# A gate product with its tiles out of step: tile 0 ends one unit sooner, and the next row is turned amid the last unit

## The chip, the cores and the metric

The kernel runs on one core of one Trainium2 chip. Time is device time in microseconds, the median of the runs. Everything is float32; each product is made of three passes over split operands (below).

## The reference

Two stacked blocks over 256 tokens of width 1024. Block 1 has two layers. Each ends in a gated embedding, and what it gives is normed again at once by the next layer (or, after the second layer, by block 2's first feed-forward):

```python
x = x + rms_norm(ff, norm_ffn_post[i])
e = (p[i] @ w_ple_proj[i]) * jax.nn.sigmoid(x @ w_ple_gate[i])
x = x + rms_norm(e, norm_ple[i])
# next layer
h = rms_norm(x, norm_mix_pre[i + 1])
z = h @ w_in[i + 1]
```

The product `x @ w_ple_gate` is "the gate product" here, the step from one layer to the next "the seam". There are two seams.

## The kernel before

**Tiles and units.** The 256 tokens are two tiles of 128 rows, t = 0 and 1 ("rows" below are such tiles). Weights come in units of 128 x 2048 float32 (1 MB) through three slots of `raw`. ScalarE rounds a unit to its high part `whi` (`split` in ScalarE's program, L1482 and L1486), VectorE subtracts to get the low part `wlo` (`split` in VectorE's program, L2013; halves of a unit through L2019). A product is rows_high x weights_high (L660, L650), rows_high x weights_low (L629) and rows_low x weights_high (L638). TensorE's instruction for a unit and a tile is `unit_product`; for a wide unit it is 12 matmuls, four in each pass. Usually the order of the passes is high, low weights, low rows. If `rows_first` names the unit, the low rows come ahead of the low weights.

**The gate product** is `wide_job(U_PGATE, 4, ...)`: four units, each used by both tiles. The order written (t, unit) is (0,0) (0,1) (1,0) (1,1) (0,2) (0,3) (1,2) (1,3). Counted over the layer these units are 68 to 71; 72, 73, 74 and 75 are the first four units of what follows. A slot comes free for ScalarE when the last tile has used the unit three before; SyncE issues the load of a unit when the low part of the unit two before it is made.

**From gate to next row.** For each tile: sigmoid on ScalarE (`gate_e`, L1809), product with the embedding on VectorE (`embed`, L2484), then beside each other a square sum on ScalarE (`square_e`, L1519) and a product with the row of gains of the next norm on VectorE (`embed_rows`, L2489). Of tile 1 the last quarter of that product is made by GpSimd (L2893). GpSimd makes the inverse root from the sum (L2775 addition, L2776 power). VectorE combines all to the next normed row in `ht` (`next_row`, L2499). TensorE transposes it (`turn`, L698, eight transposes for a tile), ScalarE copies out the high part (L1494), VectorE the low part (L2019).

**Order around the seam.** Every engine's order is written out by hand. After the gate product TensorE does three filler transposes (`stay_warm`, L705), the turn of tile 0 of the next row, and six more fillers. Then it begins the next layer's first product. The turn of tile 1 lies inside that product: in the first layer's successor at the second unit, in the middle of its low-weight pass, after five and a half passes; in block 2's first product, whose second unit keeps the usual order of passes, after four and a half. Behind this turn TensorE waits for the whole of unit 73's low part. Its first half has a flag of its own (`seam_lo`).

VectorE's order: splits of units 70, 71 and 72 with small work between; `embed(0)`, `embed_rows(0)`, `next_row(12, 0)`; first half of 73; `embed(1)`, `embed_rows(1)`; low part of tile 0's next row; `next_row(13, 1)`; second half of 73; the residual of tile 0 (`add_embedded`); low part of tile 1's next row; half of 74; residual of tile 1; half of 74; 75.

Of the kernel before, what the change touches and what calls it, by code (L numbers as in the profile page):

```python
# [21 lines left out]
P = 128  # L22
S = 256
T = S // P
D = 1024
# [26 lines left out]
SLOTS = 3  # L52
UW = 2048
# [10 lines left out]
ACT = mybir.ActivationFunctionType  # L64
# [56 lines left out]
START_POS = START_COL + DT  # L121
START_FREQ = START_POS + T
START_WORDS = START_FREQ + ROPE // 2
WARM_SHORT, WARM_LONG, WARM_START = 6, 3, 10
AHEAD_ONE, AHEAD_TWO = 6, 3


# [133 lines left out]
def two_blocks(nc, A, out):  # L261
    ctx = ExitStack()
    with ctx:
# [12 lines left out]
        xs = sb("xs", [P, T, D])  # L276
# [107 lines left out]
        def sem(name):  # L384
            if name not in sems:
                sems[name] = ctx.enter_context(nc.semaphore(name))
            return sems[name]
# [22 lines left out]
        def u_view(buf, u, kts, cols):  # L410

            return buf[:, u % SLOTS, 0:kts * cols].rearrange("p (k n) -> p k n", k=kts)
# [184 lines left out]
        def _(pe):  # L597
            w = Place()

            def free_before(cls, k):  # L600

                _, name, n = w.read(cls, k - 2)
                pe.wait_ge(sem(name), w.at(name, n))
# [70 lines left out]
            def unit_product(u, t, kt, parts, start, stop, ready=None, by_halves=False):  # L674


                ready = ready or AT_ONCE
                if t == 0:
                    if by_halves:
                        pe.wait_ge(sem("first_hi"), w.at("first_hi", u + 1))  # L680
                    elif ready.seam:
                        unit_hi_there(u)
                    else:
                        unit_there(u)
                ready.before(t, kt)
                return product(parts, start, stop,
                               weights_lo=(lambda: low_weights_there(u, ready)) if t == 0 and ready.seam else None,
                               amid=lambda i: ready.amid(t, kt + i), rows_lo=lambda: ready.rest(t, kt), rows_first=kt in ready.rows_first and t == 0,
                               half=(lambda: unit_hi_there(u)) if t == 0 and by_halves else None,
                               by_turns=w.layer == 0 and t == 0 and by_halves)  # L690
# [16 lines left out]
            def rows(k, name, n, src=None, ahead=AHEAD_TWO, first_turned=False, rows_first=(), in_parts=None,  # L707
                     part_there=None, second_turned=False):

                src = ht if src is None else src
                turned = [first_turned, second_turned]

                def turn_half(g):
                    turned[0] = True
                    turn(k + g, lambda j: src[:, 0, (4 * g + j) * P:(4 * g + j + 1) * P], 4)

                def turn_tile(t):
                    if not turned[t]:  # L720
                        turned[t] = True
                        pe.wait_ge(sem(name), w.at(name, n + t + 1))
                        for g in range(2):
                            turn(k + 2 * t + g, lambda j: src[:, t, (4 * g + j) * P:(4 * g + j + 1) * P], 4)

                def before(t, kt):
                    if kt == 0:
                        turn_tile(t)
                    if kt % 4 == 0:
                        turn_hi_there(k + 2 * t + kt // 4)  # L730

                def amid(t, kt):
                    if kt == ahead:
                        turn_tile(1)
                        if in_parts is not None and t == 0:
                            unit_there(in_parts)

                def rest(t, kt):
                    if kt % 4 == 0:
                        was_read("turn", k + 2 * t + kt // 4)  # L740
                turn_tile.half = turn_half
                return Ready(before, amid, rest, True, rows_first, in_parts, part_there), turn_tile

            def wide_job(u, units, hf, hi, lo, ready=None, late=None):

                for j0 in range(0, units, 2):
                    for t in range(T):
                        for j in range(j0, min(j0 + 2, units)):  # L750
                            if j == 0:
                                free_before("half", hf + t)
                            if late and (j, t) == (units - 1, T - 1):
                                late()
                            vh, vl = u_view(whi, u + j, 2, D), u_view(wlo, u + j, 2, D)
                            outs = [ps[:, 4 + 2 * t + n, :] for n in range(2)]
                            last = unit_product(u + j, t, 2 * j,
                                                [(outs, hi[:, 2 * j + k, t * P:(t + 1) * P], lo[:, 2 * j + k, t * P:(t + 1) * P],
                                                  [vh[:, k, n * 512:(n + 1) * 512] for n in range(2)],
                                                  [vl[:, k, n * 512:(n + 1) * 512] for n in range(2)]) for k in range(2)],  # L760
                                                j == 0, j == units - 1, ready)

                            if j == units - 1:
                                last.then_inc(sem("half_done"), 1)
                            elif t == T - 1:
                                last.then_inc(sem("used"), 1)

            def ffn(u, gu, tn, hf, ready, between=None, by_columns=False):
                def gate_up(u, gu, ready=None):
# [259 lines left out]
            def layer1():  # L1029
# [206 lines left out]
                                   True, True, amid=(lambda i: turn_first(0) if i == 1 else None) if t == 0 else None)  # L1236
                    last.then_inc(sem("half_done"), 1)
                was_read("half", HF_PROJ)
                ready_embed, turn_embed = rows(TN_PLE, "x_ready", 2, xs)
                ffn(U_FFN, 0, TN_HID, HF_DOWN, ready, lambda: turn_embed(0))  # L1240
                wide_job(U_PGATE, 4, HF_PG, act_hi, act_lo, ready_embed)
                stay_warm(WARM_LONG)
                rows(len(TURN1) + TN_MIX, "h_ready", PER_LAYER["h_ready"])[1](0)
                stay_warm(WARM_SHORT)

            for n, s in enumerate(counted[0::2]):
                pe.sem_inc(s, BASE)
# [213 lines left out]
        def _(act):  # L1461
# [165 lines left out]
            def layer1():  # L1627
# [174 lines left out]
                square_half(11, HF_DOWN + 1, fold[:, 1:2])  # L1802
                split(1)
                turned_rows_hi(TN_PLE, (1,))
                split(2)

                def gate_e(t):
                    half_there(HF_PG + t)
# [7 lines left out]
                gate_e(0)  # L1816
                square_e(12, 0)
                split(1)
                gate_e(1)
                turned_rows_hi(len(TURN1) + TN_MIX, (0,))  # L1820
                square_e(13, 1)
                split(1)
                turned_rows_hi(len(TURN1) + TN_MIX, (1,))
# [170 lines left out]
        def _(dve):  # L1994
# [232 lines left out]
            def layer1():  # L2227
# [284 lines left out]
                nc.vector.tensor_tensor(row_next[:, :], gains[:, 0, :], gains[:, 1, :], ALU.mult)\  # L2512
                    .then_inc(sem("v_link"), 1)
                links[0] += 1
                split(1)
                embed(0)
                dve.wait_ge(sem("v_link"), w.at("v_link", links[0]))
                embed_rows(0)
                next_row(12, 0)
                u = done[0]  # L2520
                assert u == UNITS1 + 1
                dve.wait_ge(sem("hi"), w.at("hi", u + 1))
                kept = [(slice(None), u % SLOTS, slice(c * UW // 2, (c + 1) * UW // 2)) for c in range(2)]
                rest(wlo[kept[0]], raw[kept[0]], whi[kept[0]]).then_inc(sem("seam_lo"), 1)
                embed(1)
                embed_rows(1, 3 * D // 4)
                turned_rows_lo(len(TURN1) + TN_MIX, 0)
                next_row(13, 1)
                rest(wlo[kept[1]], raw[kept[1]], whi[kept[1]]).then_inc(sem("lo"), 1)
                done[0] += 1  # L2530
# [562 lines left out]
```

## Time and profile before

| | |
|---|---|
| median of 3 runs | 1860.77 us (1860.44 to 1861.28) |
| profiled execution | 1860.99 us |
| its span, first to last instruction | 1859.2 us |
| granted TensorE clock, mean | 0.999 |
| TensorE, VectorE, ScalarE, GpSimd busy | 99%, 65%, 53%, 9% |

The profile is of one execution. Its lines give start, length and engine; PE is TensorE's matmuls, PEld its weight loads, DVE VectorE, ACT ScalarE, POOL GpSimd, SP SyncE. Times in brackets are idle time in front of an instruction and who ended it. A gap between weight loads tells when TensorE could go on better than the matmuls' modelled ends do.

### The profile page before, as it was taken

To read this page: it belongs to the slowest core of one execution; us is meant where nothing else is said; L and a number is where in the kernel's file an instruction comes from. 1 tells how busy PE (TensorE), PEld (TensorE's weight loads), DVE (VectorE), ACT (ScalarE), POOL (GpSimd) and SP (SyncE) were. 2 spreads that over 40 slices of the span, in tenths; PEclk is the share of its full clock that TensorE was granted. 3 is DMA by queue.
4 is the path that set the end of the run, shared out by engine and by line. 5 is a ranking of instruction groups with operands and counts; after the bars stand their busy time and mean duration, and the time that the engine had idled before them with its cause. 6 is when DMAs were issued, how large, how long until landed. Compare 5 with 4: busy or idle time off the path is not lost.

```text
span 1859.2 us, 26803 instructions
## 1 busy us (share of the span) xinstructions
PE 1847.4 (99%) x9608; PEld 1544.2 (83%) x9608; DVE 1209.4 (65%) x1493; ACT 991.3 (53%) x1299; POOL 161.7 (9%) x260
## 2 busy tenths in 40 slices
PE   9999999999999999999999999999999999999998
PEld 7878888888877888888888887788888888778887
DVE  7875665668876666667755646666666556576555
ACT  6774454456675454445544556644454444575443
POOL 8100010002210010000100021000020000100000
PEclk9999999999999999999999999999999999999999
DMA  7345566554435465555556454465565555535553
GB/s 260 111 155 189 179 204 203 194 181 156 155 121 187 170 215 201 179 185 192 189 201 203 165 196 149 154 203 184 181 200 183 182 199 192 182 114 171 184 188 113
DMA packets 204724, 333.18 MB, mean 179 GB/s; under 512 B 10976, under 2 KB 149856, under 8 KB 204640
## 3 DMA queue, kind: packets, MB, share of 16 engines
q1 hardware_dynamic: 201376, 320.82, 51.5%
q0 software_dynamic: 3120, 11.02, 1.8%
q8 instruction: 48, 0.79, 0.2%
q14 instruction: 36, 0.29, 0.0%
q10 hardware_dynamic: 144, 0.26, 0.0%
HBM read 331.01 MB, written 1.05 MB: 179 GB/s over the span
## 4 chain that ended last, share of the span: by engine, by line
PE 96%; DVE 1%; DMA 1%; issue 1%; ACT 0%; POOL 0%; SPq 0%; POOLq 0%; DVEq 0%; ACTq 0%
PE ps L819 21%; PE ps L660 19%; PE ps L638 19%; PE ps L629 19%; PE ps L837 11%; PE ps L698 3%; PE ps L930 2%; PE ps L942 2%; PE ps L958 2%; DMA raw<-w_in_dram 1%; DVE eb L2484 0%; POOL stat L2776 0%; DVE wlo L2019 0%; PE ps L795 0%; ACT prob L1519 0%
## 5 line engine op out<-in xcount | busy, mean ns | idle before, releaser
L2013 DVE TENSOR_TENSOR wlo<-raw,whi 128x2048 fp32r<-128x2048 f32 (+1 forms) x294 | 664.4, 2260 | 180.4 <-ACT whi L1486 176.6
L1486 ACT ACTIVATE whi<-raw 128x2048 fp32r<-128x2048 f32 (+3 forms) x306 | 569.7, 1862 | 136.2 <-PE ps L638 133.2
L819 PE MATMUL ps<-act,whi 128*128 128x512 f32 x1728 | 403.6, 390 | 0.0
L819 PEld LDWEIGHTS ps<-act,whi 128*128 128x128 f32 x1728 | 323.5, 188 | 66.5
L1549 ACT ACTIVATE hid<-ps 128x512 f32<-128x512 f32 x54 | 32.2, 597 | 396.1 <-PE ps L837 396.1
L2085 DVE TENSOR_TENSOR hid<-ps,hid 128x512 f32<-128x512 f32 x54 | 37.4, 692 | 314.1 <-ACT hid L1549 314.1
L837 PEld LDWEIGHTS ps<-act,wlo 128*128 128x128 f32 x1728 | 214.5, 192 | 4.2
L837 PE MATMUL ps<-act,wlo 128*128 128x256 f32 x1728 | 215.8, 283 | 0.0
L629 PE MATMUL ps<-wlo,act 128*128 128x512 f32 (+2 forms) x768 | 207.6, 385 | 0.8 <-DVE wlo L2013 0.7
L660 PE MATMUL ps<-whi,act 128*128 128x512 f32 (+2 forms) x760 | 201.9, 386 | 0.2
L638 PE MATMUL ps<-whi,act 128*128 128x512 f32 (+2 forms) x760 | 198.7, 381 | 0.6 <-DVE act L2019 0.6
L638 PEld LDWEIGHTS ps<-whi,act 128*128 128x128 f32 x760 | 140.1, 188 | 28.9 <-DVE act L2019 1.4
L629 PEld LDWEIGHTS ps<-wlo,act 128*128 128x128 f32 x768 | 139.7, 188 | 29.1 <-DVE wlo L2013 1.4
L660 PEld LDWEIGHTS ps<-whi,act 128*128 128x128 f32 x760 | 138.4, 188 | 27.6 <-issue 0.8
L2775 POOL TENSOR_TENSOR stat<-stat,eps 128x1 f32<-128x1 f32 x43 | 23.3, 542 | 1438.1 <-ACT prob L1519 1437.9
L660 PE MATMUL ps<-whi,hid_hi 128*128 128x512 f32 x496 | 134.5, 393 | 0.0
L629 PE MATMUL ps<-wlo,hid_hi 128*128 128x512 f32 x496 | 133.4, 390 | 0.0
L638 PE MATMUL ps<-whi,hid_lo 128*128 128x512 f32 x496 | 132.7, 389 | 0.0
L629 PEld LDWEIGHTS ps<-wlo,hid_hi 128*128 128x128 f32 x496 | 93.0, 188 | 19.9
L638 PEld LDWEIGHTS ps<-whi,hid_lo 128*128 128x128 f32 x496 | 93.1, 188 | 19.4
L660 PEld LDWEIGHTS ps<-whi,hid_hi 128*128 128x128 f32 x496 | 89.2, 189 | 15.3
L1541 ACT ACTIVATE hid_hi<-hid 128x512 fp32r<-128x512 f32 x54 | 34.2, 632 | 70.5 <-PE ps L638 70.5
(267 smaller groups left out, 1958.7 us busy)
## 6 DMA issues: line engine op xcount, KB each, us to landing
raw<-ffn_w_gate_dram SPq DMA_DIRECT2D x88, 512.0 KB, 3.7
raw<-ffn_w_up_dram SPq DMA_DIRECT2D x88, 512.0 KB, 4.7
raw<-ffn_w_down_dram SPq DMA_DIRECT2D x88, 512.0 KB, 4.3
raw<-w_in_dram SPq DMA_DIRECT2D x62, 512.0 KB, 4.5
raw<-w_ffn_gate_dram SPq DMA_DIRECT2D x44, 512.0 KB, 3.7
raw<-w_ffn_up_dram SPq DMA_DIRECT2D x44, 512.0 KB, 4.7
raw<-w_ffn_down_dram SPq DMA_DIRECT2D x44, 512.0 KB, 4.4
raw<-a_w_qkv_dram SPq DMA_DIRECT2D x24, 512.0 KB, 4.3
```

What stands on the lines that cost most here:

```text
L629: last = nc.tensor.matmul(o, hi, a, start=False, stop=last_pass and stop and i == len(parts) - 1)
L638: last = nc.tensor.matmul(o, lo, a, start=False, stop=last_pass and stop and i == len(parts) - 1)
L660: nc.tensor.matmul(o, hi, a, start=start and i == 0, stop=False)
L698: last = nc.tensor.transpose(bank[0:rows, j * P:(j + 1) * P], src(j), ident[:, :])
L819: nc.tensor.matmul(ps[:, 2 * g + j, :], vh[:, k, g, j * P:(j + 1) * P], both[:, 4 * half + k, :, :], start=half == 0 and k == 0, stop=False)
L837: last = nc.tensor.matmul(ps[:, 2 * g + j, 0:S], vl[:, k, g, j * P:(j + 1) * P], act_hi[:, 4 * half + k, :], start=False, stop=half == 1 a ...
L930: return nc.tensor.matmul(ps[:, sc % 2, t * S:t * S + cols], q[t], k[:, 0:cols], start=True, stop=True)
L942: last = nc.tensor.transpose(ps[:, bank, kt * S + t * P:kt * S + (t + 1) * P], prob[:, sc % PROBS, t, kt * P:(kt + 1) * P], ident[:, :])
L958: return nc.tensor.matmul(o, v[:, kt], probT[:, sc % 2, kt, c0:S], start=kt == 0, stop=kt == T - 1)
L1486: nc.scalar.activation(whi[:, u % SLOTS, half:words], raw[:, u % SLOTS, half:words], ACT.Copy)\
L2013: nc.vector.tensor_tensor(wlo[:, u % SLOTS, 0:words], raw[:, u % SLOTS, 0:words], whi[:, u % SLOTS, 0:words].bitcast(F32), ALU.subtract)\
L2085: nc.vector.tensor_tensor(dst[:, :, :], ps[:, 2 * g:2 * g + 2, 0:S], dst[:, :, :], ALU.add)\
```

## The change

- **The gate product's order** becomes (0,0) (0,1) (1,0) (0,2) (0,3) (1,1) (1,2) (1,3), passed as `order`. Tile 0 is done after five unit products instead of six, and three of tile 1 follow. For the product of unit 3 with tile 0 the low rows go ahead of the low weights (`rows_first=(6,)`).
- **TensorE's seam**: all nine fillers go. Tile 0 of the next row is turned in the middle of the low-weight pass of the last product.
- **ScalarE**: unit 73 is split in two instructions, one ahead of the copies of the turned tile 0, one behind the sigmoid of tile 1. The sigmoid of tile 0 comes ahead of the split of unit 72, and the sigmoid of tile 1 behind the copies of tile 0.
- **VectorE**: the split of unit 72 moves behind `next_row` of tile 0, followed by the low part of tile 0's next row. The first half of unit 73 moves from ahead of `embed(1)` to behind it.

TensorE:

```diff
-WARM_SHORT, WARM_LONG, WARM_START = 6, 3, 10
+WARM_START = 10
...
-            def wide_job(u, units, hf, hi, lo, ready=None, late=None):
-                for j0 in range(0, units, 2):
-                    for t in range(T):
-                        for j in range(j0, min(j0 + 2, units)):
-                            if j == 0:
-                                free_before("half", hf + t)
...
+            def wide_job(u, units, hf, hi, lo, ready=None, late=None, order=None):
+                by_two = [(t, j) for j0 in range(0, units, 2) for t in range(T) for j in range(j0, min(j0 + 2, units))]
+                for t, j in order or by_two:
+                    if j == 0:
+                        free_before("half", hf + t)
...
-                ready_embed, turn_embed = rows(TN_PLE, "x_ready", 2, xs)
+                ready_embed, turn_embed = rows(TN_PLE, "x_ready", 2, xs, rows_first=(6,))
                 ffn(U_FFN, 0, TN_HID, HF_DOWN, ready, lambda: turn_embed(0))
-                wide_job(U_PGATE, 4, HF_PG, act_hi, act_lo, ready_embed)
-                stay_warm(WARM_LONG)
-                rows(len(TURN1) + TN_MIX, "h_ready", PER_LAYER["h_ready"])[1](0)
-                stay_warm(WARM_SHORT)
+                turn_next = rows(len(TURN1) + TN_MIX, "h_ready", PER_LAYER["h_ready"])[1]
+
+                def turn_amid_last(t, kt):
+                    ready_embed.amid(t, kt)
+                    if (t, kt) == (1, 7):
+                        turn_next(0)
+
+                wide_job(U_PGATE, 4, HF_PG, act_hi, act_lo,
+                         Ready(ready_embed.before, turn_amid_last, ready_embed.rest, True, ready_embed.rows_first),
+                         order=((0, 0), (0, 1), (1, 0), (0, 2), (0, 3), (1, 1), (1, 2), (1, 3)))
```

ScalarE:

```diff
-                split(2)
+                split(1)
+
+                def split_half(c):
+                    u = done[0]
+                    if c == 0:
+                        act.wait_ge(landed[u % SLOTS], w.at(f"landed{u % SLOTS}", 32 * (u // SLOTS + 1)))
+                        name, k = w.end_of(u - SLOTS)
+                        act.wait_ge(sem(name), w.at(name, k))
+                    part = slice(c * UW // 2, (c + 1) * UW // 2)
+                    nc.scalar.activation(whi[:, u % SLOTS, part], raw[:, u % SLOTS, part], ACT.Copy)\
+                        .then_inc(sem("hi" if c else "first_hi"), 1)
+                    done[0] += c
...
                 gate_e(0)
                 square_e(12, 0)
                 split(1)
+                split_half(0)
+                turned_rows_hi(len(TURN1) + TN_MIX, (0,))
                 gate_e(1)
-                turned_rows_hi(len(TURN1) + TN_MIX, (0,))
+                split_half(1)
                 square_e(13, 1)
```

VectorE:

```diff
-                split(1)
                 embed(0)
                 dve.wait_ge(sem("v_link"), w.at("v_link", links[0]))
                 embed_rows(0)
                 next_row(12, 0)
+                split(1)
+                turned_rows_lo(len(TURN1) + TN_MIX, 0)
+                embed(1)
                 u = done[0]
                 assert u == UNITS1 + 1
                 dve.wait_ge(sem("hi"), w.at("hi", u + 1))
                 kept = [(slice(None), u % SLOTS, slice(c * UW // 2, (c + 1) * UW // 2)) for c in range(2)]
                 rest(wlo[kept[0]], raw[kept[0]], whi[kept[0]]).then_inc(sem("seam_lo"), 1)
-                embed(1)
                 embed_rows(1, 3 * D // 4)
-                turned_rows_lo(len(TURN1) + TN_MIX, 0)
                 next_row(13, 1)
```

## Rows read from the trace of the kernel before

**Rows 1.** The page's first part: busy us (share of the span) x instructions.

```profile
PE 1847.4 (99%) x9608; PEld 1544.2 (83%) x9608; DVE 1209.4 (65%) x1493; ACT 991.3 (53%) x1299; POOL 161.7 (9%) x260
```

**Rows 2.** Timeline of the first seam, weight loads of TensorE: start, length, engine, line.

```profile
442.81 0.48 PEld L705 LDWEIGHTS ps<-ident 128*128 128x128 f32 x3
...
443.63 0.86 PEld L698 LDWEIGHTS ps<-ident,h 128*128 128x128 f32 x8 [0.34 <-DVE h L2499]
...
445.11 0.76 PEld L660 LDWEIGHTS ps<-whi,act 128*128 128x128 f32 x4
...
447.50 0.77 PEld L638 LDWEIGHTS ps<-whi,act 128*128 128x128 f32 x4 [0.70 <-DVE act L2019]
```

**Rows 3.** Timeline of the second seam, transposes amid a product.

```profile
886.36 0.42 PEld L629 LDWEIGHTS ps<-wlo,act 128*128 128x128 f32 x2
...
886.82 1.03 PEld L698 LDWEIGHTS ps<-ident,h 128*128 128x128 f32 x8
...
888.19 0.89 PEld L638 LDWEIGHTS ps<-whi,act 128*128 128x128 f32 x4
```

**Rows 4.** Timeline ahead of the first seam: splits, end of tile 0, first row.

```profile
431.59 2.29 DVE L2013 TENSOR_TENSOR wlo<-raw,whi 128x2048 fp32r<-128x2048 f32 x1 [1.40 <-ACT whi L1486]
...
436.07 2.29 DVE L2013 TENSOR_TENSOR wlo<-raw,whi 128x2048 fp32r<-128x2048 f32 x1
...
437.38 0.87 PEld L660 LDWEIGHTS ps<-whi,act 128*128 128x128 f32 x4
...
441.44 0.18 POOL L2775 TENSOR_TENSOR stat<-stat,eps 128x1 f32<-128x1 f32 x1 [16.39 <-ACT prob L1519]
...
442.30 1.28 DVE L2499 SCALAR_TENSOR_TENSOR h<-eg,stat,xg 128x1024 f32<-128x1024 f32 x1 [0.95 <-POOL stat L2776]
```

**Rows 5.** Timeline of the first seam, the second row.

```profile
443.24 1.03 ACT L1809 ACTIVATE eb<-ps 128x1024 f32<-128x1024 f32 x1
...
443.50 1.22 DVE L2019 TENSOR_TENSOR wlo<-raw,whi 128x1024 fp32r<-128x1024 f32 x1
...
444.63 1.22 DVE L2484 TENSOR_TENSOR eb<-eb,gate 128x1024 f32<-128x1024 f32 x1
...
445.89 0.96 DVE L2489 TENSOR_TENSOR eg<-eb,row_next 128x768 f32<-128x768 f32 x1
...
445.93 1.51 POOL L2893 TENSOR_TENSOR eg<-eb,row_next 128x256 f32<-128x256 f32 x1 [3.67 <-DVE eb L2484]
...
448.26 1.29 DVE L2499 SCALAR_TENSOR_TENSOR h<-eg,stat,xg 128x1024 f32<-128x1024 f32 x1 [0.21 <-POOL stat L2776]
...
450.58 1.02 PEld L698 LDWEIGHTS ps<-ident,h 128*128 128x128 f32 x8
```

**Rows 6.** Timeline of the next layer's first products.

```profile
459.11 0.30 PEld L629 LDWEIGHTS ps<-wlo,act 128*128 128x128 f32 x2 [0.27 <-DVE wlo L2019]
...
462.39 0.76 PEld L629 LDWEIGHTS ps<-wlo,act 128*128 128x128 f32 x4 [0.22 <-DVE wlo L2013]
...
463.72 1.35 DVE L2013 TENSOR_TENSOR wlo<-raw,whi 128x1152 fp32r<-128x1152 f32 x1
```

**Rows 7.** Timeline, VectorE and GpSimd at once: at 38 us, then at 454 us.

```profile
38.31 1.72 DVE L2013 TENSOR_TENSOR wlo<-raw,whi 128x1152 fp32r<-128x1152 f32 x1 [0.73 <-ACT whi L1486]
...
454.25 1.22 DVE L2019 TENSOR_TENSOR wlo<-raw,whi 128x1024 fp32r<-128x1024 f32 x1
...
454.48 1.04 POOL L2775 TENSOR_TENSOR stat<-stat,eps 128x1 f32<-128x1 f32 x1 [6.25 <-ACT prob L1519]
```

**Rows 8.** Loads of the seam from issue to landing, for SyncE's line.

```profile
DMA to landing us min/median/max: 2.9/4.1/5.2
```

**Rows 9.** Windows at the end, engines in the order PE, PEld, DVE, ACT, POOL; then PEclk.

```profile
1852.00:1853.00 1.00, 0.69 (x4) 0.23 (x2) 0.96 (x2) 0.60 (x2) 0.00 (x0) 1.00 0.44 176
...
1856.00:1857.00 1.00, 0.00 (x0) 0.00 (x0) 0.00 (x0) 0.23 (x1) 0.00 (x0) 0.68 0.13 45
...
1857.00:1858.00 1.00, 0.00 (x0) 0.00 (x0) 0.00 (x0) 0.00 (x0) 0.00 (x0) 0.50 1.02 387
```

More of the change, by code:

```diff
@@ L742, in rows @@
                 return Ready(before, amid, rest, True, rows_first, in_parts, part_there), turn_tile
-            def wide_job(u, units, hf, hi, lo, ready=None, late=None):
-                for j0 in range(0, units, 2):
-                    for t in range(T):
-                        for j in range(j0, min(j0 + 2, units)):
-                            if j == 0:
-                                free_before("half", hf + t)
[L753 to L766, printed above, removed]
@@ new lines, in wide_job @@
+            def wide_job(u, units, hf, hi, lo, ready=None, late=None, order=None):
[3 more added lines that the diff above has]
+                        free_before("half", hf + t)
+                    if late and (j, t) == (units - 1, T - 1):
+                        late()
+                    vh, vl = u_view(whi, u + j, 2, D), u_view(wlo, u + j, 2, D)
+                    outs = [ps[:, 4 + 2 * t + n, :] for n in range(2)]
+                    last = unit_product(u + j, t, 2 * j,
+                                        [(outs, hi[:, 2 * j + k, t * P:(t + 1) * P], lo[:, 2 * j + k, t * P:(t + 1) * P],
+                                          [vh[:, k, n * 512:(n + 1) * 512] for n in range(2)],
+                                          [vl[:, k, n * 512:(n + 1) * 512] for n in range(2)]) for k in range(2)],
+                                        j == 0, j == units - 1, ready)
+                    if j == units - 1:
+                        last.then_inc(sem("half_done"), 1)
+                    elif t == T - 1:
+                        last.then_inc(sem("used"), 1)
```

## The prediction

> **What bounds the kernel now.** The busy time by engine comes first: TensorE is busy for 99% of the span [rows 1], so time is won only by taking work or waits off TensorE. At the end of a block-1 layer both lie close together. I then read the timeline around the seam between the layers, where the weight loads tell when TensorE can go on. A unit product is 12 matmuls in three passes of four; from 437.38 to 442.81 six passes go by, 5.43 us, so a pass takes 0.905 us and a product 2.715 us [rows 2, 4]. At X = 442.81 the gate product ends. Until the next layer's first pass at 445.11 there are 2.30 us: three filler transposes, a wait of 0.34 us, eight transposes of the next row, six fillers (not shown). Two passes on, TensorE waits another 0.70 us for the low part of that row [rows 2]. The second seam, 437 us later, repeats this to within 0.01 us, so everything below counts twice.
>
> The timeline of VectorE and GpSimd is the other half of the picture. From 442.30 on VectorE has one gap of 0.21 us; TensorE then stands 0.27 us and 0.22 us for low parts of weights at 459.11 and 462.39 [rows 4, 5, 6]. Behind the seam VectorE's sequence, not TensorE's work, sets the end.
>
> **What goes.** Nine fillers and the bare transposes leave the gap. Eight transposes amid a product cost 888.19 - 886.36 - 0.905 = 0.925 us [rows 3]. So 2.30 - 0.925 = 1.375 us go per seam, and the 0.70 us wait if the low part is early enough: up to 2.07 us, or 4.15 us for both.
>
> **The new order inside the product.** Counting four products back from 437.38, the first unit of tile 1 starts at 426.52 and ends at 429.24. Then come units 2 and 3 of tile 0, to 431.95 and 434.67. Unit 3's high part is there at 431.59, in time; its low part at 431.59 + 2.29 = 433.88 [rows 4]. The rows' low pass is put first, so it is wanted only at 434.67 - 0.905 = 433.76. A short wait stays; bounds are nothing and 0.2 us, I take 0.1 us. Tile 0 ends at 434.77, not 437.38.
>
> **The first row.** From tile 0's end at 437.38 to its transposes at 443.63 are 6.25 us, nearly all latency through ScalarE, VectorE and GpSimd [rows 2, 4]. Moved, the row is ready at 441.02. TensorE asks for it in the middle of the second pass of the last product, 442.81 + 0.1 - 1.5 x 0.905 = 441.55. There is no wait, 0.5 us in hand. The price of this cover failing is the difference alone. VectorE's split of unit 72, 2.29 us at 436.07 before [rows 4], now follows the row, from about 440.95 to 443.2; TensorE wants it at 444.7. ScalarE splits unit 73 in two pieces instead of one; it works in the shadow of waits, and the halves lie on either side of the gate of tile 1, so cost nothing. On SyncE's queue the load of unit 74 waits for unit 72's low part and goes out some 5 us later, at 443.2. With a landing of at most 5.2 us [rows 8] it is there by 448.9, before VectorE's and TensorE's turn for it in the fifties. Behind it on ScalarE stand the copies of the second row, wanted after 451. The load is hidden; if it took 2 us more, ScalarE would be late for that row by part of it.
>
> **The second row: where it is lost.** X moves from 442.81 to 442.81 + 0.925 + 0.1 = 443.83, because the transposes now lie ahead of it. From X the second row must still go: 0.43 us to the sigmoid, 1.06 us to VectorE's product, 3.63 us to the combining instruction, 1.33 us to TensorE [rows 5], 6.45 us in all. Before, it had 0.33 us more, since VectorE was still in a split when the sigmoid ended (443.24 + 1.03 + 0.03 against 444.63). Before, TensorE came for the row at X + 7.77 and did not wait. Now it has five and a half passes to do at the first seam, 4.98 us, and four and a half at the second, 4.07 us. It must stand there. The fillers covered a latency that stays.
>
> The order on VectorE makes this longer. Behind the product of tile 1 (end E, 445.85 before) came 0.96 us for three quarters of the next product, and GpSimd did the last quarter beside it. GpSimd's piece, issued at 445.93, ended at 447.44, 0.59 us behind the end of VectorE's at 446.85: it hardly moved while VectorE read two tensors [rows 5]. Likewise a 0.18 us addition took 1.04 us and ended 0.05 us behind a VectorE subtraction that began before it [rows 4, 7]. Now VectorE goes from the product straight into half a split, 1.22 us, and then the 0.96 us. Three ways are open. From the piece's end to the combining instruction went 0.82 us (447.44 to 448.26), 0.67 us of it behind a small addition of 0.18 us. GpSimd comes in between the two (the small addition did, with another VectorE instruction right behind) and holds VectorE up: piece done at E + 1.72, the three quarters at about E + 2.55, addition at E + 2.60, combining at E + 3.3. Before it was E + 2.4, so 0.90 us late. Or GpSimd comes last: E + 2.0 + 0.59 + 0.82 = E + 3.42, 1.02 us. Or it comes between and holds nothing up, the addition being stretched alone: E + 2.05 + 0.67, 0.33 us. A split of 128x1152 with a GpSimd instruction under way at its start, at 38.31, took 1.72 us instead of 1.35 us [rows 6, 7], so VectorE is held up; I take 0.95 us, between the first two ways. The lowest bound is nothing at all, if the engines don't touch here.
>
> The Trainium skill, in SBUF — State Buffer, section "Who interferes with whom", says that a VectorE instruction with two SBUF inputs and a GpSimd instruction that reads SBUF exclude each other, whichever came first going first. By that rule the term is 0.9 to 1.0 us, by free overlap nothing; the stretched rows agree with the rule.
>
> **The sum for one seam.** Start of the combining instruction for row two: 0.925 (transposes) + 0.1 (short wait) - 0.33 (VectorE is free now) + 0.95 (GpSimd) = 1.65 us later. What VectorE does from there (row, half a split, residual, low parts, units 74 and 75) it does as before, one after the other, and TensorE was waiting on the last of it already. So TensorE's 462.39 becomes about 464.0. TensorE's own saving shows earlier and is spent in waits: about 2.4 us for the row at the first seam, about 3.3 us at the second (some 0.3 us of it for the half split just ahead). At the second seam the transposes came at 886.82 with only 0.1 us in hand [rows 3], so the same 1.65 us holds. Twice is 3.3 us. The profiled execution takes 1860.99 us (span 1859.2 and 1.8 around it), so 1864.3; against the median of 1860.77 us it is **1864.0**, 0.17% slower. A counter-check by VectorE's work: the row's combining ends at 440.95, then 2.2 us of split, then the 15.5 us that lay between 443.5 and 459.1, and two new idle stretches of 0.9 us each: 460.5, 1.5 us behind.
>
> **Rivals.**
> - No contention: GpSimd is not held up by the new neighbour (term between 0 and 0.33 us). Then a seam costs 0.7 to 1.0 us, the time is 1862.2 to 1862.8. Against it stand the stretched rows. 12%.
> - TensorE's clock falls in the new stand. At the end the last matmul is over at 1852.7, the clock is full until 1856 and averages 0.68 of 2.4 GHz in 1856 to 1857, then 0.50, the 1.2 GHz level [rows 9]. The stands here are shorter, 2.4 and 3.0 us in one piece, so for a fall they are short, though nothing rules it out. Passes then take 1.8 us, not 0.905; three or four such passes cost about 3 us more each time, less where VectorE sets the pace: 1866 to 1869. 10%. The Trainium skill, TensorE: Matmul & The Clock Gate, section "HAM oscillation — how this bites in real kernels", says that gaps between bursts of matmuls take the clock to its lower level; no stand of this size follows full work in the trace of before.
> - The second row is no bound and the whole saving stays: 4.15 us less, 1856.6, 0.22% faster. It needs the row ready 4.1 to 5.0 us behind X; by the sum it is ready 7.4 us behind (6.45 + 0.95), and even without GpSimd's part 6.45 us. The change begins to gain once that chain is under 7.4 - 1.65 = 5.75 us, and gains all at 4.1 us. 5%.
> - The change does about nothing, because something hides VectorE's lateness: within 1 us of 1860.8. 5%.
> - As forecast, with each term at its bounds (0.85 to 0.95, 0 to 0.2, 0.9 to 1.02): 1.4 to 1.85 us a seam, 1863.6 to 1864.5. 68%, and the own range of this case is 1863.3 to 1864.9.
>
> **Numbers.** 0.2% is 3.7 us, about what a measurement tells from no change, and the forecast of 3.3 us lies just inside it. Of the likeliest case about a third passes that line, with the clock case 33% slower. Faster by over 0.2% is 5%, the rest 62%. The range 1861.5 to 1866.0 leaves out the faster cases and the greater part of the clock case.
>
> **What would show it.** TensorE's count falls by 18. The low part of the first row is waited for no more. The transposes of the second row begin about 1.35 us behind the combining instruction and have an idle of over 2 us before them, released by VectorE. GpSimd's quarter takes 1.7 to 2.6 us instead of 1.51. VectorE has two new idle stretches, before the product of tile 1 and before the combining. Granted clock 1.00 in both seams. The forecast is wrong if the quarter ends 0.6 us behind the product, if the first row is late, or if unit 3 is waited for by over 0.3 us.

## The result and the profile after

The changed kernel takes 1865.09 us (median of 14 runs, 1863.51 to 1866.48) against 1860.64 us for the kernel before on the same chips (14 runs, 1860.15 to 1861.28). The ratio is 1.0024, with a 95% interval of 1.0017 to 1.0031: slower by 4.45 us, or 0.24%. The forecast was 1864.0, 0.17% slower, in a range of 1861.5 to 1866.0, with 33% on slower by over 0.2%. The profiled execution takes 1864.91 us, 3.92 more than the profiled one of before.

The page's first part, after. TensorE has 18 instructions fewer than in [rows 1] and as much work otherwise:

```profile
PE 1846.8 (99%) x9590; PEld 1543.3 (83%) x9590; DVE 1210.3 (65%) x1493; ACT 990.5 (53%) x1299; POOL 162.4 (9%) x260
```

The timeline of the first seam, after (start, length, engine, line). VectorE's lines are 18 higher than before: L2031 is the split (L2013 before), L2037 subtractions through the helper (L2019), L2502 `embed` (L2484), L2507 `embed_rows` (L2489), L2517 `next_row` (L2499); GpSimd's quarter is L2911 (L2893):

```profile
431.24 2.29 DVE L2031 TENSOR_TENSOR wlo<-raw,whi 128x2048 fp32r<-128x2048 f32 x1 [1.40 <-ACT whi L1491]
...
433.59 0.77 PEld L629 LDWEIGHTS ps<-wlo,act 128*128 128x128 f32 x4 [0.23 <-DVE wlo L2031]
...
439.32 1.28 DVE L2517 SCALAR_TENSOR_TENSOR h<-eg,stat,xg 128x1024 f32<-128x1024 f32 x1 [0.95 <-POOL stat L2794]
...
441.21 1.02 PEld L698 LDWEIGHTS ps<-ident,h 128*128 128x128 f32 x8
...
443.48 0.87 PEld L660 LDWEIGHTS ps<-whi,act 128*128 128x128 f32 x4
...
444.96 1.23 DVE L2502 TENSOR_TENSOR eb<-eb,gate 128x1024 f32<-128x1024 f32 x1 [0.96 <-ACT eb L1825]
...
446.10 1.22 DVE L2037 TENSOR_TENSOR wlo<-raw,whi 128x1024 fp32r<-128x1024 f32 x1
...
446.27 1.65 POOL L2911 TENSOR_TENSOR eg<-eb,row_next 128x256 f32<-128x256 f32 x1 [6.98 <-DVE eb L2502]
...
447.24 1.49 DVE L2507 TENSOR_TENSOR eg<-eb,row_next 128x768 f32<-128x768 f32 x1
...
447.89 0.89 POOL L2793 TENSOR_TENSOR stat<-stat,eps 128x1 f32<-128x1 f32 x1
...
449.44 1.28 DVE L2517 SCALAR_TENSOR_TENSOR h<-eg,stat,xg 128x1024 f32<-128x1024 f32 x1 [0.71 <-POOL stat L2794]
...
450.78 0.85 PEld L698 LDWEIGHTS ps<-ident,h 128*128 128x128 f32 x8 [2.35 <-DVE h L2517]
...
454.97 0.76 PEld L638 LDWEIGHTS ps<-whi,act 128*128 128x128 f32 x4 [0.91 <-DVE act L2037]
```

What is to be seen, beside [rows 2, 4, 5]. This execution is 0.35 us ahead when it reaches the seam (431.24 against 431.59), so 0.35 us is added to its times in every comparison.

- Unit 3 is waited for a little at 433.59, 0.23 us in the row; the next product starts at 434.40 + 0.35 = 434.75, 0.1 us later than before. The first row is combined at 439.32 and turned at 441.21 with no wait.
- The gate product ends at 443.48 + 0.35 = 443.83, 1.02 us later than X before. The nine fillers and the 0.70 us wait are gone.
- Tile 1's embedding product ends at 446.19 + 0.35, 0.69 us later than before: 1.02 us less the 0.33 us.
- Behind it GpSimd's quarter takes 1.65 us and VectorE's three quarters 1.49 us instead of 0.96; the small addition 0.89 instead of 0.18. Combining begins 3.25 us behind the product's end, against 2.41 before. In all it begins 449.44 + 0.35 - 448.26 = 1.53 us later.
- TensorE stands 2.35 us at 450.78 for the second row and 0.91 us at 454.97 for its low part.

The second seam, after:

```profile
885.87 0.30 PEld L629 LDWEIGHTS ps<-wlo,act 128*128 128x128 f32 x2 [0.31 <-DVE wlo L2037]
...
887.94 1.28 DVE L2517 SCALAR_TENSOR_TENSOR h<-eg,stat,xg 128x1024 f32<-128x1024 f32 x1 [0.71 <-POOL stat L2794]
...
889.28 0.86 PEld L698 LDWEIGHTS ps<-ident,h 128*128 128x128 f32 x8 [3.11 <-DVE h L2517]
...
891.01 1.61 PEld L638 LDWEIGHTS ps<-whi,act 128*128 128x128 f32 x4
...
895.00 0.89 PEld L638 LDWEIGHTS ps<-whi,act 128*128 128x128 f32 x4
```

Here the stand is 3.11 us, with a shorter one of 0.31 us just ahead. Then the loads behind it are stretched: the four loads of the pass at 891.01 take 1.61 us instead of 0.88. The windows say why (columns: length of the window, then PE, PEld, DVE, ACT and POOL busy with counts, the granted clock, the DMA engines' share, GB/s):

```profile
889.00:890.00 1.00, 0.72 (x7) 0.72 (x8) 1.00 (x2) 0.02 (x1) 0.00 (x0) 1.00 0.00 0
890.00:891.00 1.00, 0.98 (x5) 0.64 (x4) 1.00 (x2) 1.00 (x2) 0.00 (x0) 0.61 0.00 0
891.00:892.00 1.00, 1.00 (x4) 0.80 (x3) 0.96 (x2) 0.06 (x1) 0.00 (x0) 0.50 0.60 123
892.00:893.00 1.00, 1.00 (x4) 0.81 (x3) 1.00 (x2) 0.07 (x1) 0.00 (x0) 0.50 0.85 287
893.00:894.00 1.00, 1.00 (x4) 0.77 (x4) 1.00 (x3) 1.00 (x2) 0.00 (x0) 0.68 1.02 418
```

The granted clock is full during the stand and falls just behind it, to 0.50, the level of 1.2 GHz. From the means of the windows (0.61, 0.50, 0.50, 0.68) it is low for about 3.4 us. In the first seam it is 1.00 throughout.

The account of the profiled execution needs four more lines. A split of a unit in the second layer's gate product, before and after:

```profile
868.72 2.29 DVE L2013 TENSOR_TENSOR wlo<-raw,whi 128x2048 fp32r<-128x2048 f32 x1 [0.85 <-ACT whi L1486]
```

```profile
869.76 2.29 DVE L2031 TENSOR_TENSOR wlo<-raw,whi 128x2048 fp32r<-128x2048 f32 x1 [1.42 <-ACT whi L1491]
```

and, before, the combining of the second seam and the pass that begins at 895.00 after:

```profile
885.38 1.28 DVE L2499 SCALAR_TENSOR_TENSOR h<-eg,stat,xg 128x1024 f32<-128x1024 f32 x1 [0.21 <-POOL stat L2776]
...
890.96 0.87 PEld L638 LDWEIGHTS ps<-whi,act 128*128 128x128 f32 x4
```

- Ahead of the seams the execution is 0.35 us early.
- The first seam costs 1.39 us: the split is 1.04 us later than before, and 0.35 us had been in hand. That is 0.14 us less than the 1.53 us of the combining. It goes at VectorE's split of a unit that stands at 460.04 before and at 460.97 after: the idle time in front of it is 0.99 us before and 0.73 us after.
- The rest, 3.92 - 1.04 = 2.88 us, is the second seam's. There the combining begins 887.94 - 885.38 - 1.04 = 1.52 us later, as in the first. The remaining 1.4 us is the clock: the pass at 895.00 begins 4.04 us later than before, which is 1.48 us more than 1.04 + 1.52.

### The profile page after: what moved, and what is told of

Same layout as the page of the kernel before. It is cut to its first block, busy times and chain, and to the rows that moved or that the text cites. A ratio compares the mean times of both kernels' runs of the same rounds, so it can differ in the third digit from the quotient of the medians.

```text
span 1863.1 us, 26767 instructions
## 1 busy us (share of the span) xinstructions
PE 1846.8 (99%) x9590; PEld 1543.3 (83%) x9590; DVE 1210.3 (65%) x1493; ACT 990.5 (53%) x1299; POOL 162.4 (9%) x260
## 4 chain that ended last, share of the span: by engine, by line
PE 96%; POOL 2%; DVE 1%; issue 0%; ACT 0%; DMA 0%; POOLq 0%; DVEq 0%; ACTq 0%
PE ps L818 21%; PE ps L629 19%; PE ps L638 19%; PE ps L660 19%; PE ps L836 11%; PE ps L698 3%; PE ps L929 2%; PE ps L941 2%; PE ps L957 2%; POOL stat L2794 0%; POOL stat L2793 0%; DMA prob<-start_dram 0%; POOL eg L2911 0%; POOL hid L2966 0%; POOL hid L2967 0%
## 5 line engine op out<-in xcount | busy, mean ns | idle before, releaser
L2031 DVE TENSOR_TENSOR wlo<-raw,whi 128x2048 fp32r<-128x2048 f32 (+1 forms) x294 | 664.4, 2260 | 180.7 <-ACT whi L1491 177.2
L1491 ACT ACTIVATE whi<-raw 128x2048 fp32r<-128x2048 f32 (+2 forms) x304 | 567.2, 1866 | 137.1 <-PE ps L638 135.1
```

What stands on the lines that cost most here:

```text
L1491: nc.scalar.activation(whi[:, u % SLOTS, half:words], raw[:, u % SLOTS, half:words], ACT.Copy)\
L2031: nc.vector.tensor_tensor(wlo[:, u % SLOTS, 0:words], raw[:, u % SLOTS, 0:words], whi[:, u % SLOTS, 0:words].bitcast(F32), ALU.subtract)\
```

## The experiments

Each was timed against the kernel before, beside it on the same chip. Where two medians of experiments are set against each other, they are from such pairs; the kernel before gave 1860.45 us in the first four and 1860.63 us in the last four. Of the 14 runs of the changed kernel's own timing, two have a span of 1861.7 us and twelve have 1862.8 to 1863.4 us. The gap between the groups is of the size of the clock's price below, so the clock probably fell in nearly all of them and not in each. Only one of them has a trace, and it is of the larger group.

### Fillers in the stand

```diff
 def amid(t, kt):
     if kt == ahead:
+        if t == 0 and warm:
+            stay_warm(warm, 5)
         turn_tile(1)
...
-                             part_there=seam_half_there)[0]
+                             part_there=seam_half_there, warm=16 if w.layer else 0)[0]
```

(and the same for block 2's first rows)

> The changed kernel with 16 filler transposes put where TensorE stands, ahead of the turn of the second row, at both seams. They take about 16 x 0.115 = 1.8 us of stands of 2.35 and 3.11 us. Theory (the clock fell at the second seam because of the stand, and that costs time): the granted clock stays 1.00, the second seam is 1.3 to 1.6 us shorter, the first unchanged; median about 1863.6 against 1865.1 us of the changed kernel. Rival (the slow clock costs nothing, since VectorE sets the pace behind the stand): the clock stays full, the time stays at 1865.1. Rival two (the fillers delay the turn): 0.3 us or more slower.

Measured: 1863.57 us (11 runs, 1863.22 to 1864.13), ratio to before 1.0016 (1.0007 to 1.0025), 1.5 us under the changed kernel by the medians and 1.3 us by what each adds to the kernel before on its chip, and the spread is a third of what it was. The timeline of the second seam and its window:

```profile
886.33 1.90 PEld L705 LDWEIGHTS ps<-ident 128*128 128x128 f32 x16
...
889.38 0.86 PEld L698 LDWEIGHTS ps<-ident,h 128*128 128x128 f32 x8 [1.16 <-DVE h L2519]
...
890.87 0.90 PEld L638 LDWEIGHTS ps<-whi,act 128*128 128x128 f32 x4
```

```profile
890.00:892.00 2.00, 1.96 (x11) 1.48 (x10) 1.97 (x3) 1.09 (x2) 0.00 (x0) 1.00 0.10 31
```

The fillers lie inside the stand (1.16 us of it is left), the row is turned when it was (889.38 against 889.28), the clock stays at 1.00 and the loads of a pass behind take 0.90 us. So the fall of the clock was the stand's doing, and it cost 1.3 to 1.5 us; the first rival, that VectorE's pace hides it, is out.

### The first half of unit 73 early

ScalarE splits unit 73 whole ahead of the copies of the first row (first piece of the diff); VectorE's half is ahead of the low part of the first row and of the embedding product (second piece):

```diff
-                split(1)
-                split_half(0)
+                split(2)
                 turned_rows_hi(len(TURN1) + TN_MIX, (0,))
                 gate_e(1)
-                split_half(1)
```

```diff
                 split(1)
-                turned_rows_lo(len(TURN1) + TN_MIX, 0)
-                embed(1)
...
                 rest(wlo[kept[0]], raw[kept[0]], whi[kept[0]]).then_inc(sem("seam_lo"), 1)
+                turned_rows_lo(len(TURN1) + TN_MIX, 0)
+                embed(1)
                 embed_rows(1, 3 * D // 4)
```

> The changed kernel with the first half of unit 73 split ahead of tile 1's embedding product, on both engines, so that behind that product VectorE has only its three quarters to do, as in the kernel before. Theory (GpSimd is held up by the two back-to-back VectorE subtractions and products): GpSimd's quarter takes 1.5 us instead of 1.65, its small addition 0.18 instead of 0.89 us, and the combining instruction starts 2.4 us behind the end of the embedding product instead of 3.25; 0.75 to 0.85 us less at each seam, and with a stand of 2.3 us at the second seam the clock probably stays up, 1.4 us more; median 1862.1 to 1863.6. Rival (the order on VectorE makes no difference, the latency is all ScalarE's and GpSimd's own): 1865.1.

Measured: 1862.98 us (11 runs, 1861.81 to 1864.73), ratio 1.0012 (1.0003 to 1.0022). The first seam:

```profile
445.21 1.21 DVE L2500 TENSOR_TENSOR eb<-eb,gate 128x1024 f32<-128x1024 f32 x1
...
446.45 0.96 DVE L2505 TENSOR_TENSOR eg<-eb,row_next 128x768 f32<-128x768 f32 x1
446.50 1.51 POOL L2909 TENSOR_TENSOR eg<-eb,row_next 128x256 f32<-128x256 f32 x1 [7.06 <-DVE eb L2500]
...
447.98 0.18 POOL L2791 TENSOR_TENSOR stat<-stat,eps 128x1 f32<-128x1 f32 x1
...
448.82 1.28 DVE L2515 SCALAR_TENSOR_TENSOR h<-eg,stat,xg 128x1024 f32<-128x1024 f32 x1 [1.41 <-POOL stat L2792]
```

VectorE's three quarters take 0.96 us, GpSimd's quarter 1.51, the addition 0.18, and combining begins 448.82 - 446.42 = 2.40 us behind the product: every number as in the kernel before. The runs lie in two groups, 1861.81 to 1862.20 (five) and 1862.98 to 1864.73 (six). The profiled one belongs to the upper group. In it the second seam has a stand of 2.50 us, where 2.3 had been expected, and the clock, expected to stay up, fell behind it:

```profile
887.94 0.97 PEld L698 LDWEIGHTS ps<-ident,h 128*128 128x128 f32 x8 [2.50 <-DVE h L2515]
```

```profile
889.00:892.00 3.00, 3.00 (x9) 2.35 (x8) 2.97 (x5) 1.24 (x3) 0.00 (x0) 0.50 0.61 175
```

### Both together

> Both edits together: the half of unit 73 early and 16 fillers in the stand. Theory: full clock for certain, and 0.8 us less at each seam: 1862.0 to 1862.4; what is left over the kernel before is the transposes put ahead of tile 1's end, 0.9 us, less the 0.3 us that VectorE is free sooner, at each seam. Rival (the terms share their time, one hides the other): no faster than the better of the two alone.

Measured: 1862.21 us (11 runs, 1861.76 to 1862.42), ratio 1.0009 (1.0000 to 1.0018). The granted clock is 1.00 at both seams, and the time is under that of either edit alone, so neither term hides the other. The lower group of the half put early (1861.81 to 1862.20) is as fast, as it should be if the fillers only keep the clock up. Against the version with the fillers only (1863.57 us, same chip, clock full in both) the half put early is worth 1.36 us, 0.7 a seam, where 0.8 had been expected. Of the 4.45 us, 2.7 us are gone, and about 1.8 us stay, 0.9 a seam; the terms of transposes and short wait, less VectorE's 0.33 us, said 0.7 a seam.

### The kernel before without fillers

```diff
                 wide_job(U_PGATE, 4, HF_PG, act_hi, act_lo, ready_embed)
-                stay_warm(WARM_LONG)
                 rows(len(TURN1) + TN_MIX, "h_ready", PER_LAYER["h_ready"])[1](0)
-                stay_warm(WARM_SHORT)
```

> The kernel before without its nine fillers at each seam, nothing else changed. Theory (behind the seam VectorE's sequence sets the end, the fillers stand in latency that is there anyway): 1860.3 to 1860.8 us, TensorE stands 0.8 to 1.4 us longer at the seam. Rival (a filler costs what its load takes, 0.115 us): 18 fewer are 2.1 us less, 1858.6. Rival two (they keep the clock up): the granted clock falls behind a seam and the time rises by 1 us or more.

Measured: 1860.56 us (11 runs, 1860.19 to 1860.97), ratio 1.0000 (0.9991 to 1.0009). Its first seam:

```profile
442.95 0.86 PEld L698 LDWEIGHTS ps<-ident,h 128*128 128x128 f32 x8 [0.85 <-DVE h L2497]
...
444.36 0.76 PEld L660 LDWEIGHTS ps<-whi,act 128*128 128x128 f32 x4 [0.55 <-issue]
...
446.82 0.77 PEld L638 LDWEIGHTS ps<-whi,act 128*128 128x128 f32 x4 [0.77 <-DVE act L2017]
```

Where the fillers were, TensorE now stands, 0.85 us for the row, 0.55 us for its copies, and 0.77 us for the low part. (The matmuls' own row at 444.39 names ScalarE's copies, L1492, where the load's row says "issue".) The granted clock stays at 1.00. The nine fillers cost nothing, so taking them away could win nothing. It is the surest sign that TensorE's own work does not set the time at the seam, whatever its 99% over the whole kernel.

### One line of VectorE's order, in the kernel before

```diff
-                rest(wlo[kept[0]], raw[kept[0]], whi[kept[0]]).then_inc(sem("seam_lo"), 1)
                 embed(1)
+                rest(wlo[kept[0]], raw[kept[0]], whi[kept[0]]).then_inc(sem("seam_lo"), 1)
                 embed_rows(1, 3 * D // 4)
```

> The kernel before with one line of VectorE's order moved: the first half of unit 73 behind tile 1's embedding product instead of ahead of it, as in the changed kernel. Theory (VectorE and GpSimd hold each other up there): embedding product 0.33 us sooner, GpSimd's quarter and small addition stretched as in the changed kernel (1.65 and 0.9 us), low part of the first row and combining about 1.05 us later; 2.1 us in all, 1862.5. Rival (the same work in another order on VectorE costs nothing): 1860.5.

Measured: 1862.67 us (11 runs, 1862.49 to 1863.15), ratio 1.0012 (1.0003 to 1.0021), 2.0 us over before. The first seam:

```profile
443.82 1.23 DVE L2484 TENSOR_TENSOR eb<-eb,gate 128x1024 f32<-128x1024 f32 x1 [0.72 <-ACT eb L1809]
444.96 1.22 DVE L2019 TENSOR_TENSOR wlo<-raw,whi 128x1024 fp32r<-128x1024 f32 x1
445.13 1.66 POOL L2893 TENSOR_TENSOR eg<-eb,row_next 128x256 f32<-128x256 f32 x1 [3.35 <-DVE eb L2484]
...
446.10 1.50 DVE L2489 TENSOR_TENSOR eg<-eb,row_next 128x768 f32<-128x768 f32 x1
...
446.75 0.89 POOL L2775 TENSOR_TENSOR stat<-stat,eps 128x1 f32<-128x1 f32 x1
...
448.72 1.27 DVE L2499 SCALAR_TENSOR_TENSOR h<-eg,stat,xg 128x1024 f32<-128x1024 f32 x1
```

The stretched numbers of the changed kernel appear in the kernel before from this line alone: 1.66, 1.50 and 0.89 us. So the order of VectorE's instructions beside GpSimd's is a cause of the stretching by itself. The 2.0 us are not the price of the stretching alone, though. The trace is 0.48 us ahead here, so combining begins 448.72 + 0.48 - 448.26 = 0.94 us later than before, and VectorE goes into it without idle time: it is not GpSimd's last result that is waited for. Of the 0.94 us the longer product makes 0.54. Most of the rest is idle time of VectorE, 0.72 us in front of the embedding product, where the half split had been, against 0.21 us in front of the combining before. For what the stretching costs in the changed kernel, go by the half put early: 2.40 us against 3.25.

### GpSimd's quarter on VectorE

```diff
-                embed_rows(1, 3 * D // 4)
+                embed_rows(1)
...
-                pool.wait_ge(sem("e_ready"), w.at("e_ready", 2))
-                late = slice(3 * D // 4, D)
-                nc.gpsimd.tensor_tensor(eg[:, 1, late], eb[:, 1, late], row_next[:, late], ALU.mult)\
-                    .then_inc(sem("eg_part"), 1)
```

(`next_row` no longer waits for that quarter either.)

> The changed kernel with GpSimd's quarter of tile 1's product done by VectorE, 0.27 us more for it. Theory (GpSimd and VectorE exclude each other while both read SBUF): VectorE is not held up, its product takes 1.23 us; GpSimd's small addition stands until VectorE has ended, about 2.3 us behind the embedding product; combining at 3.0 instead of 3.25 us behind it; 0.2 us less per seam, 1864.6. Rival (no exclusion, GpSimd's latency as such): the addition starts 1.3 us behind the embedding product and takes 0.18 us, combining at 2.3 us, and the time falls by 1.9 us or more.

Measured: 1864.02 us (10 runs, 1862.58 to 1864.85), ratio 1.0017 (1.0008 to 1.0027).

```profile
444.82 1.23 DVE L2502 TENSOR_TENSOR eb<-eb,gate 128x1024 f32<-128x1024 f32 x1 [0.95 <-ACT eb L1825]
...
447.10 1.22 DVE L2507 TENSOR_TENSOR eg<-eb,row_next 128x1024 f32<-128x1024 f32 x1
...
447.39 0.98 POOL L2791 TENSOR_TENSOR stat<-stat,eps 128x1 f32<-128x1 f32 x1 [8.24 <-ACT prob L1524]
...
449.03 1.28 DVE L2515 SCALAR_TENSOR_TENSOR h<-eg,stat,xg 128x1024 f32<-128x1024 f32 x1 [0.71 <-POOL stat L2792]
```

The addition of one element per partition is issued at 447.39 and ends at 448.37, 0.05 us behind VectorE's product. Combining begins 449.03 - 446.05 = 2.98 us behind the embedding product, as expected. The time fell by 1.1 us, not 0.5: in four of the ten runs (1862.58 to 1863.01) it lies 0.9 us and more under the others, and in the profiled one, which is of these four, the clock did not fall. Its stand at the second seam is 2.83 us, shorter by 0.28 us than in the changed kernel:

```profile
888.57 0.86 PEld L698 LDWEIGHTS ps<-ident,h 128*128 128x128 f32 x8 [2.83 <-DVE h L2515]
```

```profile
889.00:892.00 3.00, 2.96 (x17) 2.33 (x15) 2.96 (x3) 1.09 (x2) 0.00 (x0) 1.00 0.40 101
```

That such a stand lets the clock stay up more often would give the rest; it rests on one trace and the grouping. It is also longer than the 2.50 us behind which the clock fell with the half put early, so the length of the stand alone does not decide.

### The transposes doubled

```diff
                     if (t, kt) == (1, 7):
                         turn_next(0)
+                        stay_warm(8)
```

> The changed kernel with eight filler transposes more behind the turn amid the last product. Theory (what TensorE does ahead of tile 1's end moves the whole chain of row two by its length): 0.9 us more at each seam, the stands of TensorE as long as before; 1866.9 to 1867.3 against 1865.1. Rival (the stand behind absorbs them): no change, the stands 0.9 us shorter.

Measured: 1866.83 us (5 runs, 1866.12 to 1867.09), ratio 1.0034 (1.0021 to 1.0047), 1.7 us over the changed kernel. Its first seam:

```profile
445.54 1.23 DVE L2503 TENSOR_TENSOR eb<-eb,gate 128x1024 f32<-128x1024 f32 x1 [1.82 <-ACT eb L1826]
...
451.37 0.85 PEld L698 LDWEIGHTS ps<-ident,h 128*128 128x128 f32 x8 [2.37 <-DVE h L2518]
```

The stand is 2.37 us, as long as in the changed kernel with its 2.35, and at the second seam it is 3.12 us against 3.11. The embedding product begins 445.54 + 0.30 - 444.96 = 0.88 us later (this trace is 0.30 us ahead of the changed kernel's). What is put ahead of tile 1's end moves the whole chain. The stand behind absorbs none of it.

### A version from these: turned behind the product

The new order of units stays; the first row is turned behind the gate product, without fillers. On ScalarE unit 73 is split early and the sigmoid of tile 1 goes ahead of the copies; on VectorE the half of unit 73 is ahead of `embed(1)` and the low part of the first row behind `embed_rows(1)`:

```diff
-                    if (t, kt) == (1, 7):
-                        turn_next(0)
...
                          order=((0, 0), (0, 1), (1, 0), (0, 2), (0, 3), (1, 1), (1, 2), (1, 3)))
+                turn_next(0)
```

> A version meant to beat both: the changed kernel's order of units, but the first row is turned behind the gate product again, without fillers, so that tile 1 ends 0.925 us sooner; ScalarE takes the sigmoid of tile 1 ahead of the copies of the turned row; the first half of unit 73 is split ahead of tile 1's embedding product, and the low part of the first row is made behind it, as before. Theory: the combining instruction of row two starts 0.1 (unit 3's short wait) - 0.33 (VectorE free sooner) = 0.2 us sooner than in the kernel before, per seam; 1860.0 to 1860.4 us, full clock. Rival (TensorE, now without 1.4 us of fillers, gains all of it): 1858. Rival two (the copies behind the sigmoid hold TensorE up, and this adds to VectorE's sequence): 1861.5.

Measured: 1860.15 us (11 runs, 1859.83 to 1860.50) against 1860.63 us (28 runs, 1860.22 to 1860.95), ratio 0.9998 (0.9989 to 1.0007).

```profile
442.58 1.02 PEld L698 LDWEIGHTS ps<-ident,h 128*128 128x128 f32 x8
...
444.64 0.76 PEld L660 LDWEIGHTS ps<-whi,act 128*128 128x128 f32 x4 [1.03 <-ACT eb L1820]
...
446.94 0.76 PEld L638 LDWEIGHTS ps<-whi,act 128*128 128x128 f32 x4 [0.63 <-DVE act L2030]
...
447.70 1.28 DVE L2510 SCALAR_TENSOR_TENSOR h<-eg,stat,xg 128x1024 f32<-128x1024 f32 x1 [0.21 <-POOL stat L2787]
```

Combining of row two begins at 447.70 + 0.35 = 448.05, 0.21 us sooner than before. It is 0.48 us under the kernel before by the medians, but the spreads overlap (five of its 11 runs are above the lowest of before, 1860.22) and the interval holds no change too, so no gain over the kernel before is shown. It is faster than the changed kernel by 4.9 us, taking each against the kernel before on its chip (-0.48 and +4.45 us). TensorE still waits 1.03 us at 444.64 and 0.63 us at 446.94 for the low part. The row at 444.64 names the sigmoid, which had ended at 444.04; the matmuls' own row at 444.67 names the copies of the turned row (L1494), which now come behind it. The gate product ends at 442.58 + 0.35 = 442.93, 0.12 us behind X before, so the chain of the second row starts nearly where it did.

## Why the prediction was right, and where it was off

**What bounds.** "Behind the seam VectorE's sequence, not TensorE's work, sets the end" is shown by the kernel before without fillers, 0.1 us from before for 18 instructions fewer.

**What goes.** 1.375 us of gap and the 0.70 us wait went, as said, and came back as stands of 2.35 and 3.11 us, the second with 0.31 us more just ahead of it (forecast 2.4, and 3.3 in all).

**The new order and the first row.** Unit 3 was waited for shortly, 0.1 us in effect as forecast. The first row was in time. The later load was hidden: it was issued at 442.83 + 0.35 = 443.18 (forecast 443.2), and ScalarE's split of that unit, at 447.36, has no idle time in front of it.

**The second row.** Of the sum 0.925 + 0.1 - 0.33 + 0.95 = 1.65 us the trace shows 1.02 for the first two and 0.69 for the first three, as forecast, and 0.84 instead of 0.95 for GpSimd. The way it went was the first of the three named: GpSimd came in between and held VectorE up (1.49 us against 0.96). That way gave 0.90 us; 0.95 was taken as a value between two ways, of which the second did not happen. The estimate also took VectorE's hold to be the whole of GpSimd's piece, 0.59 us, and the trace shows 0.53. GpSimd's quarter took 1.65 us where 1.7 to 2.6 had been named. The rule of the Trainium skill (SBUF — State Buffer, "Who interferes with whom"), that the two exclude each other, fits the traces of after, of the half put early and of the one line moved in the kernel before: GpSimd's quarter takes 1.51 us with one such VectorE instruction beside it and 1.65 us with two, and VectorE's 0.96 us or 1.49 to 1.50. Per seam 1.53 us was measured against 1.65.

**Behind the second row.** The prediction had VectorE do all the rest "one after the other", so that the pass at 462.39 would come at about 464.0. It came at 463.38 + 0.35 = 463.73 and waited for nothing, since VectorE had 0.99 us of idle time in front of its split at 460.04 and a part of the delay went there. So 1.39 us of the 1.53 were left behind the first seam.

**The step that was mis-sized** is the rival "TensorE's clock falls in the new stand". It got 10%, on the argument that the clock was full for over 3 us behind the last matmul of the kernel [rows 9] and the stands are shorter. At the second seam it fell behind 3.11 us, so one long stand with full clock gave no bound for another. Its price was put at about 3 us; the runs show 1.3 to 1.5 us. The clock is low for about 3.4 us, and TensorE's work in that time takes twice as long, so half of that time is lost at the most, and it fell at one seam only. The measured 1865.09 us lies between the range of the likeliest case (up to 1864.9) and that of the clock case (from 1866), and fits neither as priced. That the stated range holds it is in part luck: the range was wide enough for a fall of the clock that the sum did not have, and 0.24% is on the side that was given 33%. Priced rightly, the clock case would have been the sum, 3.3 us, less a little, with 1.3 to 1.5 us on it; 4.45 us were measured. The Trainium skill (TensorE: Matmul & The Clock Gate, "HAM oscillation — how this bites in real kernels") had warned of such gaps between bursts. The traces of after, with 3.11 us, and of the half put early, with 2.50 us, agree with it; that of GpSimd's quarter on VectorE has a gap of 2.83 us without a fall.

**The other rivals.** No contention is out, by the stretched rows and by the half put early. The whole saving staying is out: the chain is 7.3 us (450.78 - 443.48) in the changed kernel. The sum without a fall of the clock was 3.3 us; with the clock kept up 3.1 us were measured (1863.57 - 1860.45).

## What to carry to other kernels

An engine that is busy for 99% may be filling in for another's latency at one place: take its fillers out first and see whether the time moves. Before work is drawn ahead of a point, ask what chain starts at that point; here every microsecond put ahead of it delayed the chain in full. And where a long chain runs over GpSimd, try to leave VectorE's instructions with two inputs in SBUF out of the stretch in which GpSimd has its small steps.

## What the hardware showed beyond this

- One GpSimd addition of a single element per partition took 0.18 us or 0.89 to 1.04 us, by what VectorE was doing (and 1.82 us at 460.56 in the kernel before, beside VectorE's whole split, ending 0.05 us behind it). VectorE's product of 128x768 took 0.96 or 1.49 us, by whether GpSimd's piece got in ahead of it. Two neighbours of little work cost 0.84 us of latency.
- The granted clock fell to half at or just behind the end of stands of 3.11 and 3.12 us between full work, and in one profile behind one of 2.50 us, but not in another behind 2.83 us, nor behind 2.35 us at the first seam, nor at the kernel's end, where it was full for over 3 us. It came back after about 3.4 us. Sixteen transposes of the identity in the stand held it up. What separates a stand that ends in a fall from one that does not stays open; its length alone does not.
